# Projection loop of an RWKV mixer: sums per head on four TensorE quadrants, weight rounding moved from GpSimd to ScalarE

## What is computed

```python
h = jnp.concatenate([x, dx], axis=-1) @ w_comb           # dx = x_prev - x
r, k, v, g, w_lo, a_lo = jnp.split(h, ...)
w = -softplus(-(w0 + tanh(w_lo) @ w2)) - 0.5
a = sigmoid(a0 + a_lo @ a2)
kk = k * k_k
kk = kk / maximum(norm(kk, axis=-1, keepdims=True), 1e-12)   # per head of 64
k = k * (1 + (a - 1) * k_a)
decay = exp(-exp(w))
y = wkv7_scan(r, decay, k, v, -kk, kk * a)
bonus = sum(r * k * r_k, axis=-1, keepdims=True) * v         # per head of 64
```

## Time and profile before

| what | value |
|---|---|
| median of three runs | 2486.48 us (2485.86 to 2487.64) |
| profiled execution, its own time | 2485.72 us |
| span of its records | 2482.9 us |
| mean granted TensorE clock over the span | 0.947 |
| projection loop, pair 0 to the last sums | about 60 to 539 us of the span |
| scan's first matmul | 543.2 us |
| busy in the whole span | PE 2190.2 us (88%), DVE 1329.2 (54%), POOL 1201.1 (48%), ACT 838.6 (34%) |

### The profile page before, as it was taken

One profiled execution on the slowest core, in us unless ns is written; L12 is line 12 of the kernel. 1 busy time (PEld: TensorE's weight loads), 2 busy tenths in 40 slices (PEclk: granted clock), 3 DMA queues, 4 the chain that ended last, 5 costly groups with the idle time before them and its releaser, 6 DMA issues.

```text
span 2482.9 us, 57378 instructions
## 1 busy us (share of the span) xinstructions
PE 2190.2 (88%) x22614; PEld 1847.4 (74%) x22614; DVE 1329.2 (54%) x1932; ACT 838.6 (34%) x2187; POOL 1201.1 (48%) x708
## 2 busy tenths in 40 slices
PE   6799999989999999986948989999894999798876
PEld 4698999888888888876948947777693876565655
DVE  6766666664665566655264314454316082548645
ACT  1623323335566656553021223323202111212331
POOL 1266666552233223318847802231583897775234
PEclk8899999999999999996969999999896999899998
DMA  2233334355234323422201210100121221121001
GB/s 88 87 136 145 137 144 166 143 174 96 65 70 88 88 64 69 88 90 78 93 34 69 93 51 35 34 17 34 35 92 71 99 87 43 60 76 60 18 0 68
DMA packets 158909, 197.61 MB, mean 80 GB/s; under 512 B 120992, under 2 KB 123296, under 8 KB 156448
## 3 DMA queue, kind: packets, MB, share of 16 engines
q1 hardware_dynamic: 158752, 195.25, 25.2%
HBM read 156.24 MB, written 38.99 MB: 79 GB/s over the span
## 4 chain that ended last, share of the span: by engine, by line
PE 55%; DVE 8%; issue 7%; ACT 4%; POOL 3%; DVEq 0%; ACTq 0%; POOLq 0%
PE wide L803 8%; PE wide L1233 8%; PE wide L1234 8%; PE wide L1235 8%; PE wide L1710 5%; PE wide L1819 2%; PE wide L818 2%; PE wide L1595 1%; PE wide L1775 1%; PE wide L1803 1%; PE wide L826 1%; PE wide L820 1%; PE wide L2072 1%; POOL x_w L1092 1%; DVE normed L1371 1%
## 5 line engine op out<-in xcount | busy, mean ns | idle before, releaser
L1233 PE MATMUL wide<-mixed_high,w_high_rwkv_in 128*128 128x264 f32 x720 | 212.2, 295 | 29.0 <-ACT log_decay L435 20.1
L1092 POOL TENSOR_TENSOR x_w<-n,masks 128x192 f32<-128x192 f32 x48 | 28.7, 599 | 381.5 <-ACT n L969 381.5
L1235 PE MATMUL wide<-mixed_high,w_low_rwkv_in 128*128 128x264 f32 x720 | 206.6, 287 | 0.0
L1234 PE MATMUL wide<-u_low_second,w_high 128*128 128x512 f32 x464 | 185.5, 400 | 0.0
L1257 POOL TENSOR_TENSOR w_high<-weights,con 128x1024 fp32r<-128x1024 f32 x60 | 147.5, 2458 | 73.7 <-PE wide L1235 63.8
L1350 DVE TENSOR_TENSOR sq_sum<-sq_sum,squares 128x528 f32<-128x528 f32 (+1 forms) x54 | 87.3, 1617 | 178.3 <-ACT squares L1315 178.3
L355 PE MATMUL wide<-mixed_in,weights 128*128 128x264 f32 x672 | 159.1, 395 | 13.3 <-DVE mixed_in L325 12.3
L1233 PEld LDWEIGHTS wide<-mixed_high,w_high_rwkv_in 128*128 128x128 f32 x720 | 138.2, 192 | 37.1 <-ACT log_decay L435 26.3
L1260 POOL TENSOR_TENSOR w_low<-weights,w_high 128x1024 fp32r<-128x1024 f32 x60 | 157.6, 2627 | 4.7
L355 PEld LDWEIGHTS wide<-mixed_in,weights 128*128 128x128 f32 x672 | 129.1, 194 | 40.7 <-issue 9.5
L531 POOL TENSOR_TENSOR w_high_rwkv_in<-weights,con 128x1024 fp32r<-128x1024 f32 x45 | 108.3, 2406 | 71.7 <-PE wide L1235 71.0
(11 more groups left out here) (327 smaller groups left out, 6520.5 us busy)
## 6 DMA issues: line engine op xcount, KB each, us to landing
weights<-in_stream SPq DMA_DIRECT2D x200, 512.0 KB, 3.4
forms<-form SPq DMA_DIRECT2D x16, 2020.5 KB, 6.3
forms_in<-forms SPq DMA_DIRECT2D x96, 144.0 KB, 4.5
forms_in<-forms SPq DMA_DIRECT2D x32, 288.0 KB, 4.4
gate_bonus<-forms SPq DMA_DIRECT2D x16, 576.0 KB, 4.1
r_ahat_r<-forms SPq DMA_DIRECT2D x32, 144.0 KB, 3.5
mixed<-gate_bonus SPq DMA_DIRECT2D x14, 264.0 KB, 2.1
gated<-mixed SPq DMA_DIRECT2D x14, 264.0 KB, 5.0
```

The lines of the kernel that those rows point to most:

```text
L1233: pe.matmul(dst, w[0], x[0], start=start, stop=False)
L1234: pe.matmul(dst, w[0], x[1], start=False, stop=False)
L1235: return pe.matmul(dst, w[1], x[0], start=False, stop=stop)
```

## The change

Four things:

1. Both sums per head (`head_sums`) are four 64x64 matmuls instead of two of 128x128: one per head and half, each on a different quadrant of the array. Head 0 of the first half stands in rows 0:64, and its second half goes to rows 64:128 of the second bank; head 1 the other way round. So the second bank has the heads swapped. A semaphore instruction (`sums_turn`) stands ahead of the four, and the two matmuls of head 0 count `sums_first`, which readers wait for beside the old semaphore.
2. The readers of the sums, the root on ACT (L446, now L471) and the bonus product on DVE (L518), become three instructions each (`summed_parts`): 128x264, 64x264, 64x264.
3. ACT does the rounding (`act_weights`, a copy into the rounded type) in GpSimd's place: k and r of the next pair between the root and the tanh of g, v behind the copy of k. GpSimd keeps the subtraction.
4. ACT's last pair is written out behind its loop, since it has no next pair.

```diff
+        def head_sums(pe, dst, src):
+            pe.sem_inc(s["sums_turn"], 1)
+            for hd, rows in enumerate(TWO):
+                for b in range(2):
+                    mm = pe.matmul(dst[TWO[hd ^ b], b, 0:HALF], heads[rows, hd * C:(hd + 1) * C], src[rows, PAD + b * HALF:PAD + (b + 1) * HALF],
+                                   start=True, stop=True)
+                    if hd == 0:
+                        mm.then_inc(s["sums_first"], 1)
+            return mm
+        def summed_parts(src):
+            cols = [slice(PAD + b * HALF, PAD + (b + 1) * HALF) for b in range(2)]
+            return [(slice(0, P), cols[0], src[:, 0, 0:HALF])] + [(TWO[hd], cols[1], src[TWO[1 - hd], 1, 0:HALF]) for hd in range(2)]
...
-            for b in range(2):
-                mm = pe.matmul(wide[2][:, b, 0:HALF], heads, a_sq[:, PAD + b * HALF:PAD + (b + 1) * HALF], start=True, stop=True)
-            mm.then_inc(s["kk_summed"], 1)
+            head_sums(pe, wide[2], a_sq).then_inc(s["kk_summed"], 1)
...
+        def act_weights(act, i, j):
+            before, step = ((3, i - 1), (2, i - 1), (1, i))[j]
+            ring.wait_full(act, 1 + j, i)
+            ring.wait_used(act, before, step)
+            act.activation(w_in[0][:, (1 + j) % 2, :], ring.slot(1 + j), ACT.Copy).then_inc(w_high, 1)
...
             act.activation(real(a_k), wide[2][:, :, 0:HALF], ACT.Copy).then_inc(s["k_copied"], 1)
+            if not first:
+                act_weights(act, i, 2)
...
-            act.activation(real(a_inv), wide[2][:, :, 0:HALF], ACT.Sqrt).then_inc(s["kk_rooted"], 1)
+            act.wait_ge(s["sums_first"], 4 * i + 2)
+            for rows, cols, part in summed_parts(wide[2]):
+                ins = act.activation(a_inv[rows, cols], part, ACT.Sqrt)
+            ins.then_inc(s["kk_rooted"], 1)
+            if first:
+                act.wait_ge(s["lerp"], 6 * KD)
+            if not last:
+                act_weights(act, i + 1, 0)
+                act_weights(act, i + 1, 1)
...
-            step(dve.tensor_tensor(real(f_bon), wide[3][:, :, 0:HALF], real(f_v), ALU.mult))
+            dve.wait_ge(s["sums_first"], 4 * i + 4)
+            for rows, cols, part in summed_parts(wide[3]):
+                ins = dve.tensor_tensor(f_bon[rows, cols], part, f_v[rows, cols], ALU.mult)
+            step(ins)
...
-                    ring.wait_full(pool, load, i)
-                    ring.wait_used(pool, before, step)
-                    pool.tensor_tensor(w_in[0][:, at, :].rearrange("p (k n) -> p k n", k=KD), ring.slot(load).rearrange("p (k n) -> p k n", k=KD),
-                                       ones.unsqueeze(1).to_broadcast([P, KD, P]), ALU.mult).then_inc(w_high, 1)
                     pool.wait_ge(w_high, SPLIT * i + (j + 1 - SPLIT))
```

More of the change, by code:

```diff
@@ L278, in program @@
             "diff", "lerp", "lora_loaded", "lora_low", "proj_w", "proj_a", "tanh_w", "tanh_a", "k_copied", "r_copied", "kk_squared",
-            "p_exp", "kk_summed", "kk_rooted", "v_copied", "g_tanh", "pc_copied", "rk_summed", "dve", "pool", "stored", "in_rounded", "in_rest", "in_whole")}
+            "p_exp", "kk_summed", "kk_rooted", "v_copied", "g_tanh", "pc_copied", "rk_summed", "dve", "pool", "stored", "in_rounded", "in_rest", "in_whole", "sums_first", "sums_turn")}
         def half_bias(n, pair):
@@ L372, in program @@
         LERP_OF = [("k", 2), ("r", 3), ("v", 0), ("g", 1)]
+        TWO = (slice(0, C), slice(C, P))
+        def head_sums(pe, dst, src):
[10 more added lines that the diff above has]
+            return [(slice(0, P), cols[0], src[:, 0, 0:HALF])] + [(TWO[hd], cols[1], src[TWO[1 - hd], 1, 0:HALF]) for hd in range(2)]
         def pe_pair(pe, i, first):
@@ L415, in pe_pair, with act_pair @@
             pe.wait_ge(DVE_A.sem, DVE_A.at(i, 7))
[L416 to L420, removed]
+            head_sums(pe, wide[3], a_rk).then_inc(s["rk_summed"], 1)
+        def act_weights(act, i, j):
[3 more added lines that the diff above has]
+            act.activation(w_in[0][:, (1 + j) % 2, :], ring.slot(1 + j), ACT.Copy).then_inc(w_high, 1)
+        def act_pair(act, i, first, last=False):
             if first:
@@ L526, in pool_pair @@
                 pool.wait_ge(s["lerp"], 6 * KD)
-                for j, (before, step) in enumerate(((3, i - 1), (2, i - 1), (1, i))):
+                for j in range(SPLIT):
                     load, at = 1 + j, (1 + j) % 2
-                    ring.wait_full(pool, load, i)
-                    ring.wait_used(pool, before, step)
-                    pool.tensor_tensor(w_in[0][:, at, :].rearrange("p (k n) -> p k n", k=KD), ring.slot(load).rearrange("p (k n) -> p k n", k=KD),
-                                       ones.unsqueeze(1).to_broadcast([P, KD, P]), ALU.mult).then_inc(w_high, 1)
                     pool.wait_ge(w_high, SPLIT * i + (j + 1 - SPLIT))
@@ L2444, in _ @@
             act_lora(act)
-            over_pairs(act, act_pair, act_in_parts)
+            act_pair(act, 0, True)
+            act_in_parts(act)
+            with act.Fori(1, PAIRS - 1) as i:
+                act_pair(act, i, False)
+            act_pair(act, PAIRS - 1, False, last=True)
             passes(act, act_pass)
```

## The result

| | kernel before | changed kernel |
|---|---|---|
| median, four runs each | 2486.17 us (2484.97 to 2487.64) | 2511.62 us (2511.07 to 2513.6) |
| profiled execution, span | 2485.72, 2482.9 us | 2511.16, 2509.3 us |
| mean granted clock | 0.947 | 0.942 |

The changed kernel is slower: ratio 1.0104, 95% interval 1.0086 to 1.0121. The forecast was 2483.4.

A forecast was written before the change was run, and what follows sets the result against it. PE, busy 28.12 of 29.00 us, was taken to bound the projection loop. From 2486.5 us, 2.8 and 1.0 less and 0.7 more gave 2483.4; the 8-in-10 range was 2476.5 to 2490.0.

The forecast's parts named there:

- three terms: Projection loop's sums 2.8 us less, between pair 0 and 1 1.0 less, behind the last pair 0.7 more.
- (a): Sums on PE: quadrants sharing a bank exclude each other, so each sum costs 0.35 us more; 2496.0 us, chance 0.08.
- (d): Projection loop: PE gets a new wait for DVE's last step, held by GpSimd; 8.4 us over forecast, 2491.8; chance 0.07.
- Sums: PE, kk and r k r_k sums of pairs 1 to 14: each takes 0.79 us instead of 0.89, 2.8 less.
- The price of changing shape: PE's array, switching into and out of each quadrant sum: 0.35 us together, read off existing shape changes.
- Rival (b): Sums on PE: the shape change is hidden or smaller, saving up to 0.44 us each, down to 2473.9; chance 0.20.
- rival (c): Sums on PE: semaphore instruction or four queues eat 0.10 to 0.16 us each; 2486.2 to 2487.9, chance 0.15.
- part 2: Readers in three pieces on ACT and DVE: 0.7 us of additions against 0.4 us of cover in the loop.
- Rounding and readers: ACT rounds 1024 columns in about 1.07 us; root in pieces takes about 0.95, DVE's bonus product about 1.1.
- Between pair 0 and pair 1: ACT's rounding frees DVE of GpSimd, giving 2.1 us; late weights leave PE's v start 1.0 us earlier.
- Behind the last pair: Scan's first matmul: root 0.3, table load up to 0.1, bonus 0.4 later; DMA covers 0.1, so 0.7 us more.

The follow-up runs named there:

- sums_only: Kernel before plus only the sums on four quadrants and their readers in three pieces; rounding stays on GpSimd, ACT's last pair in its loop: 2508.3 us, ratio 1.0091.
- Round_40: Kernel before plus only rounding on ACT and its last pair written out, with 40 unused semaphore increments on ACT ahead of the scan: 2487.42 us, ratio 0.9991.

## Why the prediction was wrong, point by point

**The step that failed** is the one that isn't there. The four things that change include that ACT's last pair is written out behind its loop; the sum has three terms, and none for it, and all that follows was taken as the same in both kernels. It is the same work at another place in ACT's code: the scan loop begins 38 instructions later (6 of them from parts 1 and 2, as sums_only's 272 shows), and the runs show +29 us for that where the forecast put nothing. The page of before showed that code is fetched while the kernel runs (26 packets of 8192 bytes), but not that a loop can be caught by it, so the size was not to be had from it; that ACT's list grew by 38 instructions ahead of a loop was, and it deserved to be named as an unpriced edit and to widen the range. That the loop landed on a slow place is chance: nine of the twelve places tried cost nothing. The four rivals were all about the projection loop. The chance of 0.12 for slower was made of (a) and (d), and neither came; the time came out above the range for a reason outside all of them.

**Sums (predicted 28 x 0.10 = 2.8 less).** The mechanism was right, the size a little off. The distance between the same PE instructions of two turns is 28.48 us instead of 28.64, so 0.08 a sum; the forecast was 28.44. Over the 13 turns behind pair 2 it makes 2.1 us. The price of changing shape, read off L403 and the attention layer, held: 0.37 us where 0.35 was taken.

**Rival (a)** fell: eight records of 264 columns, two heads in one bank, in 0.68 us. The Trainium skill ("TensorEngine Tiling (Array Packing)", Gotcha 1: PSUM Pressure) says that different row tiles cannot access the same PSUM bank simultaneously; this trace disagrees for 264 columns as it did for 64, with the two on different partitions of the bank. The "up to 4x" that the prediction takes from the Trainium skill (the same page, Overview) is worked out: the page lists four 64x64 tiles and a speedup of up to 2x for a dimension of at most 64. **Rival (b)** fell with the 0.08. For **rival (c)** 0.02 us a sum are left.

**Rival (d)** did not come in this kernel. In sums_only its wait came, but not by its mechanism: there the readers in pieces add 1.26 us and GpSimd 0.16, so it is the sentence of part 2, that the cover would not be enough alone, that came true. In the changed kernel these are DVE's and GpSimd's rows of one turn:

```profile
276.53 2.48 DVE L535 TENSOR_TENSOR kk<-kk,kk_inv 128x528 f32<-128x528 f32 x1
279.24 0.76 DVE L541 SCALAR_TENSOR_TENSOR form<-kk,p_cum 128x576 f32<-128x576 f32 x1 [0.23 <-DVE kk L535]
281.28 1.31 DVE L551 TENSOR_TENSOR form<-wide,form 128x264 f32<-128x264 f32 x3
...
273.70 4.75 POOL L564 TENSOR_TENSOR w_low_rwkv_in<-weights,w_high_rwkv_in 128x1024 fp32r<-128x1024 f32 x2 [3.62 <-ACT w_high_rwkv_in L439]
```

GpSimd is done at 278.45, L535 (before's L504) has the wait and ends at 279.01, L541 takes 0.76: as predicted. From the start of the kk sums (269.21) to L541's end it is 10.79 us where before it was 11.65, and that pays for the bonus product's pieces. The waits of PE between 152 and 500 us have the one old row, unchanged:

```profile
PE wide L1263 <- ACT log_decay L458: 10.5, 12, 0.9
```

**Rounding and readers.** ACT rounds 1024 columns in 1.05 us (1.07 estimated). The root in three pieces takes 1.18 us (0.95 estimated, 0.61 in one), the bonus product 1.31 (1.1 estimated, 0.70 in one):

```profile
271.36 1.18 ACT L471 ACTIVATE kk_inv<-wide 128x264 f32<-128x264 f32 x3
272.57 2.00 ACT L439 ACTIVATE w_high_rwkv_in<-weights 128x1024 fp32r<-128x1024 f32 x2
```

**Between pair 0 and pair 1 (predicted 1.0 less).** From pair 0 to pair 2, 80.69 us instead of 81.55: 0.9 less. v of pair 1 starts where the weights are ready, and not at ACT's tanh, as forecast, though the profile names ACT:

```profile
118.94 0.56 PE L1263 MATMUL wide<-mixed_high,w_high_rwkv_in 128*128 128x264 f32 x1 [9.29 <-ACT log_decay L458]
...
116.49 2.35 POOL L564 TENSOR_TENSOR w_low_rwkv_in<-weights,w_high_rwkv_in 128x1024 fp32r<-128x1024 f32 x1 [30.98 <-ACT w_high_rwkv_in L439]
```

116.49 + 2.35 = 118.84, and PE starts at 118.94. Round_40, with the old sums and readers, gains 1.5 here, so the new ones cost the difference.

**Behind the last pair (predicted 0.7 more).** From the last L403 to the scan's first matmul it is 22.55 us instead of 21.37: 1.2 more. The term was mis-sized by the readers: together they were taken 0.44 us too short.

**Together** the projection loop gives 2.1 + 0.9 - 1.2 = 1.8 us, and 3.1 was forecast; the rest of the 3.2 by which the changed kernel reached the scan earlier is there ahead of pair 0 and differs from one execution to the next. Without its stall the kernel lies 1.6 us below (2484.66) and 2.0 above (2487.01) the kernel before beside it; 3.1 less is within the first run's interval and outside the second's. So the times alone don't confirm the forecast's size; the 1.8 us are from the traces.

## What to carry to other kernels

An edit on one engine moves every loop behind it in that engine's code. Count the instructions ahead of a loop before and after; if the time moves where nothing was changed, look for idle time put down to "issue" at a loop's first instruction and for more packets on the instruction queues, and try the kernel again with some instructions that do nothing ahead of the loop. And where an engine's work is cut into pieces to save time on the one that bounds, price the pieces where nothing covers them: here two readers at the end of the loop took back more than half of what 26 sums had saved, and inside the loop only the time that GpSimd gave back to DVE covered them.

## What the runs showed of the hardware

- A jump back can cost ACT 2.5 to 4.5 us instead of 0.2, in a loop of 280 instructions, at the starts 301, 304 and 312 and at none of the nine others tried. Each such jump goes with five more packets of code of 8192 bytes.
- A stall of 3.5 us on ACT cost 4.9 us: PE idled 2.6 us of it, and its granted clock was then at the 1.2 GHz level for 3 to 7 us, which made the same work 2.3 us longer.
- Four 64x64 f32 matmuls of 264 columns run side by side on the four quadrants, two of them in each bank (four starts within 0.02 us, the next four 0.27 us later), and the change of shape costs 0.37 us, in and out together.
- A DVE instruction that starts while GpSimd works can end only with it: the same clamp took 0.43 and 2.65 us, the same product 0.71 and 2.48. The reciprocal took 3.45 us with and without GpSimd at work.
